# A mixture-of-experts stage with the row gather issued earlier and the last expert pair reordered

## The reference

```python
def _hier_moe(h, w_rg, b_rg, w_re, b_re, w_gate, w_up, w_down):
    ...
    for gi in range(N_EXPERT_GROUPS):
        hg = jnp.einsum('td,edf->tef', t, w_gate[gi])
        hu = jnp.einsum('td,edf->tef', t, w_up[gi])
        act = (jax.nn.silu(hg) * hu * combine[:, gi, :, None].astype(t.dtype)).astype(t.dtype)
        out = out + jnp.einsum('tef,efd->td', act, w_down[gi]).astype(f32)
    return out.reshape(b, s, d).astype(h.dtype)
```

## Time and profile before

| | us |
|---|---|
| median of 3 runs | 841.33 (839.35 to 846.03) |
| the profiled execution | 837.95 |
| its span, from the first to the last instruction of the trace | 836.2 |
| PE busy | 751.3 (90% of the span) |
| DVE, ACT, POOL busy | 406.3, 189.4, 163.1 |
| mean DMA rate over the span | 207 GB/s |

### The profile page before, as it was taken

The page is one execution under the profiler, slowest core; times in us unless marked ns, Lnnn a source line. Parts: engine busy times, 40 slices in busy tenths (PEclk is TensorE's granted clock), DMA queues, the critical chain, the costliest instruction groups (busy, mean ns, idle before and its releaser), DMA issues.

```text
span 836.2 us, 9526 instructions
## 1 busy us (share of the span) xinstructions
PE 751.3 (90%) x3719; PEld 503.5 (60%) x3719; DVE 406.3 (49%) x740; ACT 189.4 (23%) x335; POOL 163.1 (20%) x121
## 2 busy tenths in 40 slices
PE   5999999999999999999999997999988687979762
PEld 2987789998888788478544883444444343434320
DVE  6698865776788886642165683121111111101227
ACT  4213325553232232400000601211111111101121
POOL 4924670000224220000000023101000000002052
PEclk9999999999999999999999999999998988989885
DMA  9796322111113222442681734799988989899493
GB/s 306 286 375 155 99 75 80 51 52 51 55 49 100 51 51 64 163 150 102 235 318 50 285 118 153 314 392 365 364 339 346 397 316 417 338 368 362 172 182 121
DMA packets 61815, 172.83 MB, mean 207 GB/s; under 512 B 17058, under 2 KB 39788, under 8 KB 47946
## 3 DMA queue, kind: packets, MB, share of 16 engines
q1 hardware_dynamic: 52324, 141.79, 46.2%
q0 software_dynamic: 8752, 28.28, 10.3%
q10 hardware_dynamic: 694, 2.14, 0.6%
HBM read 155.52 MB, written 24.67 MB: 215 GB/s over the span
## 4 chain that ended last, share of the span: by engine, by line
PE 69%; DMA 17%; DVE 6%; issue 4%; POOL 2%; ACT 1%; SPq 0%; POOLq 0%; DVEq 0%
PE psum L873 30%; DMA arena<-h_rows,info 12%; PE psum L1226 7%; PE psum L1101 7%; PE psum L1150 5%; PE psum L1211 4%; PE psum L1082 3%; DMA ring<-in_w_in_dram 3%; PE psum L1169 2%; DMA arena<-y_rows,rowsU 2%; PE psum L1031 2%; PE psum L1051 1%; POOL y_rows L813 1%; PE psum L1153 1%; PE psum L981 1%
## 5 line engine op out<-in xcount | busy, mean ns | idle before, releaser
L873 PE MATMUL psum<-ring_r 128*128 128x512 f32 (+1 forms) x832 | 214.4, 345 | 4.1 <-DVE arena_r L1638 1.7
L873 PEld LDWEIGHTS psum<-ring_r 128*128 128x128 f32 x832 | 145.3, 191 | 25.3 <-issue 3.9
L873 PE MATMUL psum<-arena_r,ring_r 128*128 128x512 f32 (+1 forms) x416 | 141.0, 376 | 0.0
L1326 ACT COPY arena<-psum 128x512 f32<-128x512 f32 (+4 forms) x104 | 57.8, 579 | 290.0 <-PE psum L1108 110.5
L1211 PE MATMUL psum<-ring,arena 128*64 128x512 f32 x512 | 114.4, 599 | 4.2 <-issue 3.0
L738 POOL TENSOR_TENSOR ring_r<-ring,ring_r 128x2048 fp32r<-128x2048 f32 x16 | 73.9, 4622 | 204.3 <-ACT ring_r L1326 204.2
L873 PEld LDWEIGHTS psum<-arena_r,ring_r 128*128 128x128 f32 x416 | 79.2, 190 | 13.7 <-issue 0.5
L1211 PEld LDWEIGHTS psum<-ring,arena 128*64 128x64 f32 x512 | 40.1, 139 | 74.5 <-issue 73.1
L1226 PE MATMUL psum<-ring,arena 128*64 128x512 f32 x256 | 67.2, 672 | 9.3 <-issue 9.3
L1150 PE MATMUL psum<-arena 128*128 128x256 f32 x256 | 63.7, 396 | 1.4 <-DVE arena L1998 1.4
L813 POOL DMA_INDIRECT y_rows<-arena,storeU x15 | 15.1, 1007 | 239.0 <-DVE arena L2116 239.0
(11 more groups left out here) (280 smaller groups left out, 917.4 us busy)
## 6 DMA issues: line engine op xcount, KB each, us to landing
ring<-in_w_exp_down_dram SPq DMA_DIRECT2D x32, 1024.0 KB, 8.4
ring<-in_w_exp_gate_dram SPq DMA_DIRECT2D x32, 1024.0 KB, 8.9
ring<-in_w_exp_up_dram SPq DMA_DIRECT2D x32, 1024.0 KB, 9.4
ring<-in_w_in_dram SPq DMA_DIRECT2D x18, 1024.0 KB, 5.3
y_rows<-arena POOLq DMA_DIRECT2D x12, 1024.0 KB, 16.9
ring<-in_w_out_ssd_dram SPq DMA_DIRECT2D x4, 1024.0 KB, 4.9
ring<-in_w_out_dram SPq DMA_DIRECT2D x4, 1024.0 KB, 5.0
arena<-in_w_ple_gate_dram SPq DMA_DIRECT2D x4, 1024.0 KB, 9.1
```

The costliest lines, as they stand in the source:

```text
L873: t = mm(o, a, b, start=(first and j == 0), stop=(last and j == 2))
L1326: return nc.scalar.copy(dst, src)
```

## The change

It does four things.
1. On POOL, for p = 1 to 13, `rows_fetched(p+2)` stands ahead of the waits for the two copies of pair p and of its store; for p = 0 it stays behind the store.
2. The overflow loop on PE, ACT and DVE stands ahead of the last pair: PE now leaves its pair loop after `down(14)`.
3. The last pair has a function of its own, `last_gate_up`: first the product with the gate slices into bank 1, then with the up slices into bank 0, each with its own signal; tanh and the first of DVE's two products run when the gate part is done, the second when the up part is.
4. On SP the last pair's slices are issued as gate, gate, up, up in place of gate, up, gate, up.

```diff
@@ -633,16 +633,14 @@
-                for half in range(2):
-                    for w, t in ((0, wg), (1, wu), (2, wd)):
-                        if 3 * half + w not in places:
-                            continue
-                        slot = expert_slot(p % 2, half, w)
-                        if p < 2:
-                            name, value = MOE_FREED[slot]
-                            sp.wait_ge(sems[name], value)
-                        src = t[p * 2 + half].rearrange("(p k) f -> p k f", p=P)
-                        sp.dma_start((ringN if w == 2 else ring)[:, slot], src).then_inc(slot_in[slot], 16)
+                for place in places:
+                    half, w = divmod(place, 3)
+                    slot = expert_slot(p % 2, half, w)
+                    if p < 2:
+                        name, value = MOE_FREED[slot]
+                        sp.wait_ge(sems[name], value)
+                    src = (wg, wu, wd)[w][p * 2 + half].rearrange("(p k) f -> p k f", p=P)
+                    sp.dma_start((ringN if w == 2 else ring)[:, slot], src).then_inc(slot_in[slot], 16)
@@ -667,7 +665,7 @@
                 sp.wait_ge(s_gu_mm, p - 1)
-                weights_in(p, (0, 1, 3, 4))
+                weights_in(p, (0, 1, 3, 4) if p < LAST else (0, 3, 1, 4))
                 sp.wait_ge(s_y_mm, p - 1)
@@ -808,13 +806,15 @@
                         pool.dma_start(dst, aps[name].broadcast_to([P, D])).then_inc(s_ln_in, 16)
+                if 0 < p < LAST - 1:
+                    rows_fetched(p + 2)
                 pool.wait_ge(s_y_act, p + 1)
                 pool.wait_ge(s_y_dve, p + 1)
                 g.indirect_dma_start(
                     out=y_dram, out_offset=bass.IndirectOffsetOnAxis(ap=storeU[:, p:p + 1], axis=0), in_=eout[:, p % 2, :],
                     in_offset=None, bounds_check=ROWS - 1, oob_is_err=False).then_inc(y_st[p % 2], 16)
-                if p + 2 <= LAST:
-                    rows_fetched(p + 2)
+                if p == 0:
+                    rows_fetched(2)
             for parity in range(2):
@@ -1212,6 +1212,19 @@
+            def last_gate_up():
+
+                pe.wait_ge(s_xgT_sb, 2 * PAIRS)
+                pe.wait_ge(s_eact_sb, LAST)
+                for w, signal in ((0, s_last_aT), (1, s_last_y)):
+                    for half in range(2):
+                        expert_slot_in(pe, LAST // 2, 1, half, w)
+                    for k in range(KD):
+                        for half in range(2):
+                            t = mm(psum[sides[half], 1 - w, 0:FF], xgT[1][:, k, sides[half]],
+                                   ring[:, expert_slot(1, half, w), k, :], start=(k == 0), stop=(k == KD - 1))
+                    t.then_inc(signal, 1)
+
             def down(p, former, parity, copied, signal):
@@ -1228,7 +1241,10 @@
             def act_t(p, parity, before, signal):
-                pe.wait_ge(s_eact_sb, p + 1)
+                if signal is s_last_aT:
+                    pe.wait_ge(s_last_aT, 4)
+                else:
+                    pe.wait_ge(s_eact_sb, p + 1)
                 if not (isinstance(p, int) and p == 0):
@@ -1257,10 +1273,8 @@
                     ple_half(n, half)
-                if 0 < p < LAST:
+                if p:
                     rows_turned_in(p + 1)
-                if p == LAST:
-                    break
                 if p == 0:
@@ -1304,9 +1318,10 @@
+            last_gate_up()
             act_t(LAST, LAST % 2, LAST, s_last_aT)
-            down(LAST, LAST // 2, LAST % 2, (s_last_aT, 2), s_last_y)
-            pe.wait_ge(s_last_y, 3)
+            down(LAST, LAST // 2, LAST % 2, (s_last_aT, 6), s_last_y)
+            pe.wait_ge(s_last_y, 4)
             for i in range(NT):
@@ -1556,14 +1569,15 @@
                     rows_copy(j + PAIRS, 0, False)
-                    hidden_tanh(j + PAIRS, 0)
+                    hidden_tanh((s_gu_mm, j + PAIRS), 0, s_tanh_sb)
                     act_copy((s_aT_mm, j + LAST + 1), 0, s_aT_sb)
                     rows_turned(more_rowsT, (s_more_rows, j * 3 + 2), s_more_rows)
                     out_copy((s_y_mm, j + LAST + 1), 16 * (PAIRS // 2), 0, s_y_act)
                 act.nop()
-            act_copy((s_last_aT, 1), LAST % 2, s_last_aT)
-            out_copy((s_last_y, 1), 16 * (LAST // 2), LAST % 2, s_last_y)
+            hidden_tanh((s_last_aT, 1), LAST % 2, s_last_aT)
+            act_copy((s_last_aT, 5), LAST % 2, s_last_aT)
+            out_copy((s_last_y, 2), 16 * (LAST // 2), LAST % 2, s_last_y)
             for i in range(2):
@@ -2076,6 +2090,16 @@
+            def last_hidden():
+
+                dve.wait_ge(s_last_aT, 2)
+                by_k = lambda t: t.rearrange("p (n k) -> p n k", k=2)
+                e = eact_wide[:, 1]
+                v.scalar_tensor_tensor(e, by_k(eth[:, 1, :]), 1.0, by_k(psum[:, 1, 0:FF]), ALU.add, ALU.mult).then_inc(s_last_aT, 1)
+                dve.wait_ge(s_last_aT, 3)
+                dve.wait_ge(s_last_y, 1)
+                v.tensor_tensor(e, e, by_k(psum[:, 0, 0:FF]), ALU.mult).then_inc(s_last_aT, 1)
+
             def hidden(p, u):
@@ -2149,14 +2171,15 @@
                     v.tensor_scalar(rowf, rowf, -float(2 * CAP), None, ALU.add).then_inc(s_weighted, 1)
-                    hidden(j + PAIRS, 0)
+                    hidden(j + LAST, 0)
                     out_half((s_y_mm, j + LAST + 1), 16 * (PAIRS // 2), 0, s_y_dve)
                     for i in range(NT):
                         dve.wait_ge(y_gath[i], 32)
                         added(i, (s_more_mm, j * 4 + i + 1), s_more_added)
                 dve.nop()
-            out_half((s_last_y, 1), 16 * (LAST // 2), LAST % 2, s_last_y)
+            last_hidden()
+            out_half((s_last_y, 2), 16 * (LAST // 2), LAST % 2, s_last_y)
             for i in range(NT):
                 dve.wait_ge(y_gath[i], 32)
                 added(i, (s_last_mm, i + 1), s_last_added)
```

More of the change, by code:

```diff
@@ L1250, in combine @@
                 t.then_inc(signal, 1)
-            for p in range(PAIRS):
+            for p in range(LAST):
                 q = p // 2
@@ L1291, in _ @@
                     gate_up(j + PAIRS // 2, 0, j * 2 + 2 * PAIRS + 2)
-                    act_t(j + PAIRS, 0, j + LAST, s_aT_mm)
+                    act_t(j + LAST, 0, j + LAST, s_aT_mm)
                     pe.wait_ge(s_more_rows, j * 3 + 1)
@@ L1510, in rows_copy, with hidden_tanh @@
                     copy(xgT[buf][:, 4 * b:4 * b + 4, :], src.rearrange("p (k t) -> p k t", k=4)).then_inc(s_xgT_sb, 1)
-            def hidden_tanh(p, u):
-                act.wait_ge(s_gu_mm, p + 1)
-                A(eth[:, u % 2, :], psum[:, u % 2, 0:FF], ACT.Tanh, scale=0.5).then_inc(s_tanh_sb, 1)
+            def hidden_tanh(made, u, signal):
+                act.wait_ge(*made)
+                A(eth[:, u % 2, :], psum[:, u % 2, 0:FF], ACT.Tanh, scale=0.5).then_inc(signal, 1)
             def act_copy(turned, u, signal):
@@ L1534, in _ @@
             ple_tanh(EARLY - 1)
-            for p in range(PAIRS):
+            for p in range(LAST):
                 q = p // 2
-                hidden_tanh(p, p % 2)
-                if 0 < p < LAST:
+                hidden_tanh((s_gu_mm, p + 1), p % 2, s_tanh_sb)
+                if p:
                     rows_copy(p + 1, (p + 1) % 2, False)
-                if p == LAST:
-                    break
                 for n in ple_done(p, 0):
```

## The result

The changed kernel takes 805.04 us (median of 4 runs, 803.48 to 806.74) against 840.34 us (4 runs, 836.9 to 846.03): a ratio of 0.957, 95% interval 0.952 to 0.963. Profiled execution against profiled execution it is 806.74 against 837.95, so 31.2 us less where the sum gave 22.6.

What follows compares the result with a forecast made beforehand. Bound by the gather circle (18.5 to 18.9 us a pair), then the weight stream (17.6), then PE (16.1). `down(14)` 26.6 us earlier, less 4 back, takes 22.6 off 837.95: 815 us, range 806 to 828.

Steps and rivals of the forecast that it cites:

- the sum: Whole kernel: `down(14)` 26.6 us earlier, less 4 us back at the end, so 22.6 us off 837.95.
- The gather circle: Pair loop: copies, store, gather and turning wait in a circle, 18.5 us a pair; early gathers would wait for nothing.
- The stream's work: Weight queue from 545 us: 219.0 us of full work, 17.6 us a pair; share 0.99 from 605, last landing 768.6.
- PE's own pace: PE without gather waits: 16.9 us for pairs 2 to 5, 16.1 for 6 to 13, reaching pair 14's product at 742.4.
- From that product to the end of `down(14)`: PE, pair 14: 7.05 us for the product, then 9.3 us to the end of `down(14)`, at 761.5.
- What comes back at the end: Store of pair 14 lands beside the weight stream: 4 us lost again, bounds 0 and 7.
- The overflow loop and the last pair: PE's end: loop of 5.95 us ahead of the last product, chain 1.2 us longer; cost zero, gathers being later.
- The order of the slices: Last pair, gate ahead of up: wins nothing, as its slices land before its product starts; cost zero, between -1 and +2.
- A: Weight stream does not speed up: pauses of 7.2% stay, last landing at 781, 828 us; chance 0.17.
- C: Early gathers slow the weight stream: at 330 GB/s the last landing is at 806, 853 us; chance 0.03.
- B: PE's clock drops after slice waits of 1.5 us: mean 18.2 us a pair, 5 us lost, 820 us; chance 0.15.
- D: Gathers still come late, over 17 us in the full stream, so the circle stays: 838 us; chance 0.05.

Runs made afterwards that it cites:

- part 1 alone: The kernel before with only the gathers moved ahead of the copies and stores; overflow loop, last pair and slice order as before: 804.21 us, ratio 0.955.

## Why the prediction was right in kind and too small

**The gather circle.** Right. "It waits for nothing": no PE wait for a gather is left, and part 1 alone gives 804.21. What was said to be late next, the stream, is what PE waits for, at pairs 12 and 13, though only there. The 10.2 us of landing was near the longest of the gathers before (6.5 to 10.9 us from 545 us on, median 7.9); the reasoning did not hang on it.

**The stream's work, the step that failed.** The prediction took 219.0 us as "full work" that only had to be pushed together, 17.6 us a pair at a share set at 0.99. This term was mis-sized: the busy share held the slow starts of a queue that had run dry, and these go with the pauses. In the changed kernel a pair's 6.29 MB take 180 x 6.29 / 68.57 = 16.5 us, at a share of 1.02, and the last slice lands at 760 in place of 768.6. The stretches with a share of 1.0 and 389 to 400 GB/s were taken for the rate of an undisturbed stream. In steps of 1 us the first of them begins with such a start, as a new batch was issued at 684.1:

```profile
685.00:686.00 1.00, 1.00 (x6) 0.90 (x5) 0.77 (x2) 0.00 (x0) 0.00 (x0) 1.00 1.46 287
```

At 690 and 695 us it reads 442. The second has a dear step too, 311 GB/s at 1.04 from 733 us on, beside a store and a gather and with no pause ahead of it. The run with `down` doubled brings the dearer MB back, the run with store and gather side by side does not. So it is shown that the cost comes with a queue that runs dry, and that steps as slow as these starts hold a good part of it, from under half to two thirds. What the engines do in that time was not tried.

**PE's own pace.** Also a term too large. 16.1 us was given to each of the pairs 6 to 13, but every other one lacks the 1.03 us product and takes 14.5, and the others take 15.6 where they wait for nothing. The pairs 2 to 5 took 16.1 and not 16.9. The product of pair 14 began at 736.75; the sum had 745.1, and 742.4 for PE by itself. So with the stream's term alone put right, the sum would have moved by 2.7 us and no more; the rest of these 8.3 us needs both terms. On the profiled executions the forecast missed by 8.6 us (31.2 against 22.6): 8.3 stand at this point, the two terms below give 1.4 back and add 1.7. In the second trace that product began at 733.31, 11.8 us ahead of the sum, and more came back at the end; such a split is good to 3 us at best.

**From that product to the end of `down(14)`.** 9.3 us in the sum, 10.7 measured (743.8 to 754.6): the wait for the last rows' matrix remained, and behind it `down` took 5.35 us and not 3.65. The same slowing as in the earlier trace rows, in a place where I had counted the fast value. Both traces have 5.35.

**What comes back at the end.** Forecast 4 us between 0 and 7, measured 2.3 in one trace and 5.0 in the other, so rightly sized. POOL waited 4.67 and 5.56 us for store 14 in place of 3.05.

**The overflow loop and the last pair.** Cost zero was right, the reason only in part. PE's chain to the combine did not grow by 1.2 us but fell from 19.9 to 17.5. The loop reads as about 7.4 us, not 5.95: PE's wait ahead of it ends with ACT's copy of the turned rows at 749.31 + 0.59 = 749.9, and the last product starts at 757.3 (in the second trace 746.5 and 753.95, 7.5 us). PE's sequencer, which reads the instructions, runs it while the matmuls of `down(14)` are still under way, so that only 2.78 us show; with one round nothing shows. The order of the slices won nothing, as forecast.

**The rivals.** A (pauses stay) and C (the stream slows down) fall with 420 GB/s over 130 us. B, the clock, showed in part. PE waited 2.1 to 3.3 us ahead of the product of pair 13 in all nine traces with early gathers and the usual `down`. In six of them the product took 8.48 to 8.79 us, in three, with waits of 2.74 and 2.76, it took 7.09. In the two traces of the changed kernel the granted clock just behind that wait was 0.53 to 0.61 in the slow case (719 to 723 us) and 1.00 in the fast one (718 to 722). It costs at most 1.7 us, once. D falls with the list of waits.

The rule of the Trainium skill, "DMA: Bandwidth & Descriptors", section "Where 436 GB/s comes from", of 358 GB/s a core from HBM does not hold for this core: the weights alone came at 385 GB/s. The two stretches that the prediction set against it, 389 and 400 GB/s, lie 9 and 12% above 358, and 7 and 10% above the mean of 365. The section "Measured (HBM→SBUF, 128 partitions, SWDGE, issued from GpSimd)" of the same page has 425 GB/s for 16 MB at once and 341 for 1 MB. Its loads were issued from GpSimd and these slices by SP, but the pattern is that of this trace: 420 with a backlog (slices still queued), less where each batch starts anew.

## What to carry to other kernels

A busy share of a DMA queue is not an amount of work: if the queue runs dry between batches, part of the busy time goes with the pauses, so divide bytes by the rate seen late in a batch and not by the mean of busy stretches. When a wait closes a circle over several engines (copy, store, gather, turning, product, copy), taking one link out can be worth the whole stage, but only down to the next bound, so work out each engine's and the stream's own pace, odd and even rounds apart. An order at the end that shortens one of two chains is worth nothing while the other is later; see which one the first common instruction waits for. And before a profile's few microseconds are shared out among causes, take a second profile of the same kernel: here it moved 3 us from one part of the path to another.

## What the runs showed of the hardware

- A queue that starts again after a pause: 98 GB/s at a share of 0.80 in the first microsecond, 442 at 1.04 two microseconds later.
- From 545 us on a gather of rows took 6.5 to 10.9 us to land in the kernel before, just behind a store, 10.3 to 11.4 with the store beside it and no pauses in the stream, 8.2 to 9.5 apart from the stores with `down` twice.
- POOL waited 7.35 and 8.09 us for the landing of store 14 when it left beside the last slices (the two runs with `down(14)` first), 4.67 and 5.56 us in the changed kernel, 3.05 when the stream was over.
- A loop of eight rounds without work took PE's sequencer some 7.4 us, part of it under matmuls that were still running.
- After a wait of 2.74 us a product took 8.48 us in place of 7.07, and after one of 2.76 us in another execution of the same kernel 7.09; after 0.29 us it took 7.09. `down(14)` behind the wait of 2.54 us took 5.35 us in both.
